# Two-layer hybrid backbone: the prologue of the first norm rewritten, with the first scale rows of the modulation computed on TensorE

## The reference, cut to what matters

```python
sc_lat = jax.nn.silu(c)
sc_ctx = jax.nn.silu(c_ctx)
for l in range(DEPTH):
    ml = adaln_chunks(sc_lat @ w_mod[l] + b_mod[l])      # 9 chunks of 1024
    mc = adaln_chunks(sc_ctx @ w_mod[l] + b_mod[l])
    xl = xl + 0.5 * ml[2] * swiglu(modulate(rms_norm(xl, norm_ffn1[l]), ml[0], ml[1]), ffn1_w13[l], ffn1_w2[l])
    xc = xc + 0.5 * mc[2] * swiglu(modulate(rms_norm(xc, norm_ffn1[l]), mc[0], mc[1]), ffn1_w13[l], ffn1_w2[l])
    ...
# modulate(h, shift, scale) = h * (1 + scale) + shift
```

## Time and profile before

| | us |
|---|---|
| median of three runs | 1928.98 |
| the profiled execution's own time | 1927.45 |
| its span in the profile | 1925.8 |
| PE busy with matmuls | 1762.3 (92%) |
| DVE busy | 1434.1 (74%) |
| ACT busy | 734.0 (38%) |

### The profile page before, as it was taken

How to read it: one execution, slowest core, us unless ns; L and a number is a source line. 1 busy time by engine, 2 the same in 40 slices (tenths; PEclk the granted TensorE clock), 3 DMA queues, 4 the chain that set the end, 5 groups by cost and what they waited for, 6 DMA issues and landing times.

```text
span 1925.8 us, 25366 instructions
## 1 busy us (share of the span) xinstructions
PE 1762.3 (92%) x9004; PEld 1444.1 (75%) x9004; DVE 1434.1 (74%) x2341; ACT 734.0 (38%) x1072; POOL 49.7 (3%) x97
## 2 busy tenths in 40 slices
PE   0699999998898898999999979999999799879999
PEld 0488888876676466788888858888887578569999
DVE  6888787887778666877777666878786778756766
ACT  3422222226646656222222262222223764654342
POOL 0000000000000000000000000000000000000000
PEclk9999999998999898999999989999999899889999
DMA  8544444422212013544444323444430321125453
GB/s 321 196 175 160 167 150 176 141 79 110 99 44 110 1 75 136 207 151 166 161 154 171 115 85 131 174 152 164 163 142 34 125 97 63 73 110 172 177 174 109
DMA packets 36859, 260.44 MB, mean 135 GB/s; under 512 B 4288, under 2 KB 5632, under 8 KB 6080
## 3 DMA queue, kind: packets, MB, share of 16 engines
q1 hardware_dynamic: 25920, 183.34, 26.4%
q0 software_dynamic: 10880, 76.32, 11.0%
HBM read 253.62 MB, written 5.24 MB: 134 GB/s over the span
## 4 chain that ended last, share of the span: by engine, by line
PE 79%; DVE 8%; ACT 8%; issue 2%; DMA 2%; POOL 0%; DVEq 0%; ACTq 0%; SPq 0%; POOLq 0%
PE ps L1304 24%; PE ps L1305 24%; PE ps L1306 24%; DVE mod_prod L856 3%; ACT n_t L543 2%; PE ps L1370 1%; ACT h_hi L546 1%; PE ps L1577 1%; DMA mod_raw<-mod_in 1%; DVE x_res L937 1%; ACT w_hi L501 1%; DVE w_lo L833 1%; PE ps L1542 1%; ACT w_hi L508 1%; DVE w_lo L838 1%
## 5 line engine op out<-in xcount | busy, mean ns | idle before, releaser
L1304 PE MATMUL ps<-h_hi,w_hi 128*128 128x512 f32 (+1 forms) x1872 | 691.8, 370 | 75.7 <-DVE h_lo L908 66.2
L1305 PE MATMUL ps<-h_lo,w_hi 128*128 128x512 f32 (+1 forms) x1872 | 686.0, 366 | 0.0
L1306 PE MATMUL ps<-h_hi,w_lo 128*128 128x512 f32 (+1 forms) x1872 | 685.3, 366 | 0.0
L1304 PEld LDWEIGHTS ps<-h_hi,w_hi 128*128 128x128 f32 x1872 | 357.6, 191 | 148.7 <-issue 71.9
L1306 PEld LDWEIGHTS ps<-h_hi,w_lo 128*128 128x128 f32 x1872 | 357.3, 191 | 58.4
L1305 PEld LDWEIGHTS ps<-h_lo,w_hi 128*128 128x128 f32 x1872 | 357.8, 191 | 56.4 <-issue 0.2
L937 DVE SCALAR_TENSOR_TENSOR x_res<-ps,abg,x_res 128x256 f32<-128x256 f32 x640 | 272.1, 478 | 155.7 <-PE ps L1306 154.9
L833 DVE TENSOR_TENSOR w_lo<-raw,w_hi 128x2048 fp32r<-128x2048 f32 x132 | 302.0, 2288 | 87.6 <-ACT w_hi L501 87.5
L501 ACT ACTIVATE w_hi<-raw 128x2048 fp32r<-128x2048 f32 x132 | 252.3, 1912 | 270.1 <-PE ps L1306 259.2
L856 DVE CUSTOM_DVE_ANT_0 mod_prod<-mod_raw,cb 128x1024 f32<-128x1024 f32 x288 | 338.7, 1220 | 15.3 <-DMA mod_raw<-mod_in 13.6
L1304 PE MATMUL ps<-a_hi,w_hi 128*128 128x512 f32 (+1 forms) x640 | 232.3, 363 | 2.2 <-DVE x_res L937 2.2
(11 more groups left out here) (189 smaller groups left out, 1322.3 us busy)
## 6 DMA issues: line engine op xcount, KB each, us to landing
raw<-ffn_in SPq DMA_DIRECT2D x132, 1024.0 KB, 4.8
mod_raw<-mod_in POOLq DMA_DIRECT2D x72, 1024.0 KB, 5.1
raw<-proj_in SPq DMA_DIRECT2D x20, 1024.0 KB, 4.9
raw<-out_w_in SPq DMA_DIRECT2D x8, 1024.0 KB, 6.5
x_spill<-x_res SPq DMA_DIRECT2D x2, 2048.0 KB, 7.2
x_res<-x_spill SPq DMA_DIRECT2D x2, 2048.0 KB, 8.1
cb<-c_in SPq DMA_DIRECT2D x2, 1024.0 KB, 4.7
x_res<-x_in SPq DMA_DIRECT2D x1, 2048.0 KB, 11.9
```

Of the source, the lines that this page charges most:

```text
L1304: pe.matmul(dst, w_hi[:, slot, wsl], hi, start=first, stop=False)
L1305: pe.matmul(dst, w_hi[:, slot, wsl], lo, start=False, stop=False)
L1306: return pe.matmul(dst, w_lo[:, slot, wsl], hi, start=False, stop=last)
```

## The change

Nothing is changed in the arithmetic of the loops. The prologue is rewritten:

- The eight scale tiles of the first norm are computed on TensorE: `scale_in` holds 8 tiles of 128 x 1024 (0.5 MB each), `scale_tile(j)` is 8 float32 matmuls with 128 x 128 weights and 2 moving columns (`cond`, Silu of 16 new columns of `cols`). They use two new half-size buffers and `sg`, `gu`.
- The eight shift tiles stay on DVE, as pieces 0 and 1 of the new `mod_in` (pieces are renumbered, there are two fewer). POOL queues: both halves of piece 0, scale tiles 0 to 3, both halves of piece 1 (each waits for half of piece 0's products), scale tiles 4 to 7. `MOD_PRE` is now pieces 2 and 3; piece 2 is computed at the end of the prologue and piece 3 in `ffn_phase(0)`. The loops have one piece for each turn as before.
- `cb` comes as one row (8 KB) and is broadcast by four float32 matmuls of 512 columns with a row of ones as weights; ACT applies Silu from PSUM.
- The sum of squares is accumulated by eight float32 matmuls with the mean matrix instead of seven DVE additions and one matmul.
- SP brings 260 columns of constants first, `x_res` in two halves, and no longer waits before the weight units. The other constants follow behind the units of FFN 0 (`const_rest`), the masks behind the write of `x_res` in the mixer; ACT rounds the masks in step `R.3` of layer 0.
- DVE takes shift, scale, root product and remainder two channel tiles at a time, with products of the later pieces between. PE takes slot 0 and slot 1 for a channel tile one behind the other (`first_pair`), scale tiles 4 to 7 between them; ACT's splits of the three slots lie inside the norm.

```diff
-            for q in range(*MOD_START):
-                load_piece(q)
+            load_half(0, 0)
+            load_half(0, 1)
+            for j in range(4):
+                load_scale(j)
+            load_half(1, 0)
+            load_half(1, 1)
+            for j in range(4, KT):
+                load_scale(j)
...
-            for slot in range(3):
-                split(slot, 0, 0)
             act.wait_ge(const_in_s, 16)
-            norm_rest(0, T)
+            norm_rest(0, T, {-1: lambda: split(0, 0, 0), 1: lambda: split(1, 0, 0), 5: lambda: split(2, 0, 0)})
...
-            dve.wait_ge(cb_ready, 2)
-            mod_pieces(0, 1)
-            for d in range(1, KT):
-                add_square(0, d, T)
-            mod_pieces(1, MOD_START[1] - 1)
-            split(0, 0, 0)
-            dve.wait_ge(cols_in_s, 16)
-            derive(0, "ab")
...
+            dve.wait_ge(cb_ready, 2)
+            products(0, 0, 0)
+            dve.wait_ge(cb_ready, 4)
+            products(0, 0, 1)
+            dve.wait_ge(cols_in_s, 16)
+            shift_half(0)
+            products(0, 1, 0)
+            products(0, 1, 1)
+            shift_half(1)
+            split(0, 0, 0)
+            scale_half(0)
+            scaled(0)
+            scaled(1)
+            dve.wait_ge(mod_put, 1)
+            products(1, 0, 0)
+            first_remainder(0)
+            first_remainder(1)
+            scale_half(1)
+            scaled(2)
+            scaled(3)
+            split(1, 0, 0)
+            first_remainder(2)
+            first_remainder(3)
+            products(1, 0, 1)
+            shift_half(2)
+            scale_half(2)
+            scaled(4)
+            scaled(5)
+            products(1, 1, 0)
+            first_remainder(4)
+            first_remainder(5)
+            products(1, 1, 1)
+            shift_half(3)
+            scale_half(3)
+            scaled(6)
+            scaled(7)
+            mod_tile(2, 0)
+            first_remainder(6)
+            first_remainder(7)
+            for j in range(1, 4):
+                mod_tile(2, j)
+            split(2, 0, 0)
...
+            def scale_tile(j):
+                pe.wait_ge(scale_in_s[j % 4], 16 * (j // 4) + 16)
...
+                for k in range(KT):
+                    last = pe.matmul(ps[:, 4 + j // 2, 2 * (j % 2):2 * (j % 2) + 2], w[:, P * k:P * k + P], cond[:, k, :], start=(k == 0), stop=(k == KT - 1))
+                last.then_inc(scale_mm, 1)
...
+            condition_rows()
+            first_mean()
+            for j in range(4):
+                scale_tile(j)
+            first_pair(0, 0)
+            first_pair(0, 1)
+            scale_tile(4)
+            scale_tile(5)
+            first_pair(1, 0)
+            first_pair(1, 1)
+            scale_tile(6)
+            scale_tile(7)
+            for k in range(2, KT):
+                for unit in range(2):
+                    first_pair(unit, k)
```

More of the change, by code:

```diff
@@ L127, in backbone @@
         lam = sb(ctx, "lam", [96])
+        cond = sb(ctx, "cond", [KT, 2])
         sel_r = sb(ctx, "sel_r", [8, P], F32R)
@@ L617, in mixer @@
                         decay_rows(layer, j)
+                        if layer == 0 and j == 3:
+                            act.wait_ge(masks_in_s, 16)
+                            act.activation(const_r[:, :], cexp[:, :, :].rearrange("p h t -> p (h t)")[:, 0:N_MASKS], ACT.Copy).then_inc(masks_done, 1)
                     elif kind == "si":
@@ new lines, in scaled, with first_remainder, products @@
+            def scaled(d):
+                dve.wait_ge(rstd_done, 2)
+                if d >= 2:
+                    dve.wait_ge(h_lo_s, d - 1)
+                tt(n_t[:, d % 2, :], x_res[:, d, :], n_rstd[:, :], ALU.mult).then_inc(t_done, 1)
+            def first_remainder(d):
+                dve.wait_ge(h_hi_s, d + 1)
+                tt(h_lo[:, d, :], n_t[:, d % 2, :], h_hi[:, d, :], ALU.subtract).then_inc(h_lo_s, 1)
+            def products(q, half, s):
+                if s == 0:
+                    dve.wait_ge(mod_in_s[half], 16 * q + 16)
+                for jj in range(2):
+                    done = 8 * q + 4 * half + 2 * s + jj
+                    if done >= 2:
+                        dve.wait_ge(mod_step, done - 1)
+                    j = 2 * half + jj
+                    dve.tensor_tensor_reduce(mod_prod[:, jj], mod_raw[:, half, jj], cb[:, s, :], 1.0, 0.0, ALU.mult,
+                                             ALU.add, mod_acc[:, s, j:j + 1]).then_inc(mod_step, 1)
+                if half == 1 and s == 1:
+                    dve.wait_ge(mod_step, 8 * q + 8)
+                    dve.tensor_copy(mod_t[:, :, 4 * q + KT:4 * q + KT + 4], mod_acc[:, :, :]).then_inc(mod_put, 1)
@@ L1615, in out_part, with condition_rows, first_mean, first_pair @@
                     x.then_inc(unit_done if m % 2 else o_mm, 1)
-            mean(0, T)
+            def condition_rows():
+                pe.wait_ge(one_s, 1)
+                pe.wait_ge(cb_in_s, 16)
+                for s in range(2):
+                    for part in range(2):
+                        pe.matmul(ps[:, 4 + 2 * s + part, :], n_rstd[0:1, 0:P], cb[0:1, s, 512 * part:512 * part + 512],
+                                  start=True, stop=True).then_inc(cond_rows, 1)
+            def first_mean():
+                pe.wait_ge(const_in_s, 16)
+                for d in range(KT):
+                    pe.wait_ge(sq_done, d + 1)
+                    pe.matmul(ps[:, 0, :], c_(K_MEAN, P), n_t[:, d % 2, :] if d else n_acc[:, :], start=(d == 0),
+                              stop=(d == KT - 1)).then_inc(mean_done if d == KT - 1 else acc_done, 1)
+            def scale_tile(j):
+                pe.wait_ge(scale_in_s[j % 4], 16 * (j // 4) + 16)
+                if j == 0:
+                    pe.wait_ge(cond_cols, 1)
+                    pe.wait_ge(cb_ready, 4)
+                w = scale_w[:, j % 4, :] if j % 4 < 2 else (sg, gu)[j % 2][:, :, :].rearrange("p s t -> p (s t)")
+                for k in range(KT):
+                    last = pe.matmul(ps[:, 4 + j // 2, 2 * (j % 2):2 * (j % 2) + 2], w[:, P * k:P * k + P], cond[:, k, :], start=(k == 0), stop=(k == KT - 1))
+                last.then_inc(scale_mm, 1)
+            def first_pair(unit, k):
+                if k == 0:
+                    split_ready(unit, 0)
+                pe.wait_ge(h_lo_s, k + 1)
+                for m in range(2):
+                    last = mm3(ps[:, 2 * unit + m, :], unit, slice(256 * k + P * m, 256 * k + P * m + P), hk(k, T), T, k == 0, k == KT - 1)
+                if k == KT - 1:
+                    last.then_inc(unit_done, 1)
+            condition_rows()
[13 more added lines that the diff above has]
+                    first_pair(unit, k)
             for layer in range(DEPTH):
```

108 lines of the change are left out of this document (74 added, 34 removed).

## The result

| | before | after |
|---|---|---|
| median of five runs, us | 1928.81 (1927.88 to 1929.27) | 1916.31 (1911.58 to 1921.08) |
| ratio, 95% interval | | 0.9937 [0.9919, 0.9955] |
| the same kernel a second time, us | | 1913.30 (1911.43 to 1921.42), 0.9918 [0.9905, 0.9932] |
| profiled execution, us | 1927.45 | 1920.51 |
| its span, us | 1925.8 | 1918.8 |

They scatter over 10 us; the five of before scatter over 1.4, and the 27 of before that were timed beside e5 over 4.4. The profiled execution is one of the slow ends of that scatter.

The account below looks back on a forecast made before the run. The prologue's DVE chain, which TensorE waits for, was taken as the bound; shortening it gives at most 26.7 us, TensorE's slow clock cuts this to 22, so 1928.98 - 22 = 1907 us, range 1900 to 1919.

Parts of the forecast that it names:

- rivals 1 and 3: 1: TensorE slow through the prologue, 1914 to 1920 us, chance 0.18; 3: transfers late, 1909 to 1915 us, chance 0.10.
- the likeliest case: Whole kernel: a gain of 22 us (18 to 25), giving 1907 us; chance 0.48.
- the point of comparison: Start of the fifth tile of `down`, 109.48 us before; what follows was taken as unchanged, so its lead is the gain.
- The rule from DVE's split of slot 0 to the fifth tile: End of prologue to fifth tile of `down`: 19.4 us, from 20.5 us before less 1.06 of waiting for TensorE.
- the rival without a stall on TensorE: Prologue: the DVE chain alone is last, a gain of 26.7 us, 1902 us; chance 0.16.
- The most it could give: DVE chain: from 29.5, 33.9 us without waiting, then 19.4, puts the fifth tile at 82.8, a gain of 26.7 us.
- 4.7 for TensorE: Prologue: TensorE's lateness in ending unit 0, between the 26.7 us of the DVE chain and the forecast gain of 22.
- the middle: TensorE in the prologue: 22 us, between a gain of 24.3 and one of 18 to 21 with early work mostly slow.
- The row that it leaned on: Prologue before: after 35 us of idleness, matmuls start 0.43 us apart from 65.39 to 71.50, a slow start costing 3.0 us.
- The other row: Mixer before: 16 small matmuls run at the fast pace, the large ones right behind them start 0.42 us apart.
- Rival 1: Prologue: TensorE stays slow, three `scale_half` steps wait 2 to 4 us each; gain 9 to 15, 1914 to 1920 us; chance 0.18.
- The wrong release: Prologue: the DMA of piece 1's first half was to release `products(1, 0, 0)` near 29.5 us, expected at 28 to 33.

Follow-up runs that it names:

- e5: The changed kernel with each scale tile one matmul instead of eight, leaving out seven eighths of the first scale's contraction: 1902.9 us, ratio 0.9863.
- e6: The kernel before with one idle DVE memset of 0.91 us ahead of its first norm products: 1929.28 us, ratio 1.0004.
- e7: The kernel before with two idle DVE memsets (1.76 and 0.91 us) ahead of its first norm products: 1931.7 us, ratio 1.0014.
- e2: The changed kernel with 64 moving columns instead of 2 in the scale tiles' matmuls, same result: 1912.66 us, ratio 0.9917.
- e8: The kernel before with only the masks' DMA and rounding moved into the mixer of layer 0: 1929.34 us, ratio 1.0001.
- e10: e9 with the first half of piece 1 queued behind two scale tiles instead of four and computed ahead of the split of slot 0: 1911.37 us, 0.9913.
- e9: e4 with the first half of x_res ahead of cols on SP, and the Silu of cond behind those of cb: 1908.48 us, 0.9901.
- e3: The changed kernel with the first half of piece 3 computed ahead of the first FFN phase's split of slot 0: 1912.62 us, ratio 0.9907.
- e12: The changed kernel with an idle DVE memset of 1.76 us ahead of derive(0, "g"): 1919.22 us, ratio 0.9955.
- e4: The changed kernel with the edits of both e2 and e3: 1908.68 us, ratio 0.9899; again 1909.68 us, 0.9898.

## Why the prediction was right, point by point

The prediction was 1907 us with 1900 to 1919; the two measurements, 1916.3 and 1913.3, lie within it, in the part that belonged to rivals 1 and 3. The sign and the mechanism held, the size of the likeliest case (a gain of 22) did not: 17.1 us at the point of comparison, 14.5 behind it, 12 to 16 at the end. Of the way from 22 to the end only the first step, to 17.1, is one that the forecast had weighed; that the losses behind it still left the time within the range is luck.

**What held.** The bound was read rightly: by e6 and e7 a delay in the prologue passes one for one to the end. For gains this held less well. By the ratio the changed kernel ends 2.3 us short of its lead at the first mixer load in one measurement and 2.3 beyond it in the other; the forms made from it that keep the full result end 3.5 to 6.4 short. The rule from DVE's split of slot 0 to the fifth tile, 19.4 us from the earlier trace rows, came out as 72.98 to 92.35, 19.37, and as 19.38 in e2. The first FFN matmul started at 35.19 (31 to 36 was given), the split of slot 0 for the norm at 27.40 with its end at 29.7 (26.5 to 30.5), the scale tiles at 1.9 to 3.55 (1.5 to 3.4). Masks and late constants cost nothing that can be seen: the lead at the first mixer load and at the write of `x_res` is the same 14.5 us, and e8 measures the masks alone. e5 is the rival without a stall on TensorE, 1902.9 us where 1902 was given. DVE's work was sized well: 33.9 us up to the end of the prologue, and in the changed kernel 36.8 from 31.21 to 68.03 with 2.9 of waiting in it. That the time agrees so closely is in part luck: e5's split of slot 0 comes at 65.7, not 63.4, its lead at the first mixer is 24.5 and not 26.7, and its layer 1 was one of the fast ones.

**The sum, term by term.** The most it could give was 26.7 us with DVE never waiting from 29.5 on. `products(1, 0, 0)` started at 31.21, 1.7 later. The three waits in `scale_half` took 2.9, and the wait for unit 0 took 4.95: 26.7 - 1.7 - 2.9 - 4.95 = 17.1, the measured lead. The forecast had put 4.7 for TensorE, where 7.8 were lost; of those e2 gives back 4.7.

**The mis-sized term: the slow level.** The forecast took "the middle" between a TensorE that recovers by itself in 15 matmuls and one that is slow to tile 4. The row that it leaned on, 6.1 us of slow matmuls behind 35 us of idleness, had only full matmuls behind it. The other row, small matmuls with slow full ones behind the earlier trace rows, was the nearer one: TensorE was at 0.50 in 30 to 40 and 45 to 50 us with no gap at all, and fell back to it in tiles 4 and 5. The Trainium skill (TensorE: Matmul & The Clock Gate, Part 1: The HAM clock gate) says that the throttled state is the default and activity releases it; the trace agrees in so far as with matmuls of 2 columns without a gap the clock fell to 0.50 and with those of 64 columns it stayed at 1.00 (25 to 30 us in e2). Rival 1 was thus the right mechanism at less than its price: it gave 9 to 15 us, since it counted 2 to 4 us for each of three waits that took 0.45, 1.14 and 1.28.

**A reading that does not stand.** The forecast took a granted clock of 1.00 beside full matmuls 0.43 us apart as a sign that the slow pace behind 35 us of idleness is not what the throttle takes. In the changed kernel full matmuls that start 0.43 apart stand beside 0.50 each time (35 to 40, 45 to 50 and 92.3 to 97.3 us). So the 1.00 of that one stretch of before is no proof of full pace; the distance between starts is the surer sign. The sum is not touched by it, since it took its prices from the starts.

**The wrong release.** The forecast let the DMA set the start of `products(1, 0, 0)`, near 29.5. The row at 31.21 has no wait: DVE came from the split of slot 0, which had waited 7.56 us for ACT behind the mean. By e10, the transfer of the half piece is there at 25.7 when it is favoured; in the changed kernel its own landing is hidden, so that it was at 31.2 or earlier is all that can be said. The mean's chain starts at 12.93, when the first half of x has landed; in the first 5 us the core moved 146 GB/s, in the kernel before 238. From then on TensorE sets the pace: ACT's fourth square waits 2.96 us for it, and each one after that 0.23 to 1.07. The first line is a window of the kernel before, the second ACT's row in the changed one:

```profile
0.00:5.00 5.00, 0.00 (x0) 1.00 0.67 238
```

```profile
17.55 0.63 ACT L557 ACTIVATE n_t<-x_res 128x512 f32<-128x512 f32 x1 [2.96 <-PE ps L1737]
```

e9, in which the order of the first transfers is another, has the same wait of 2.96 us and gains nothing.

**What was not foreseen.** First, filler work that hid a wait. Piece 4 before lay ahead of DVE's split of slot 0; the change renumbers the pieces and leaves that place empty, so the 4.95 us were idle and piece 3's products came later, whole, ahead of the update that TensorE waits for. e3 takes that back (6.9 us at the first mixer load). Second, behind the wait of 4.46 us before the fifth tile TensorE was at its slow level: it ran at full pace until 87.50, and the twelve matmuls behind the wait run at the slow pace, 0.43 us from start to start. This is the timeline of the changed kernel:

```profile
87.50 0.39 PE L1414 MATMUL ps<-a_hi,w_lo 128*128 128x512 f32 x1
...
97.21 0.63 PE L1414 MATMUL ps<-a_hi,w_lo 128*128 128x512 f32 x1
97.64 0.53 PE L1412 MATMUL ps<-a_hi,w_hi 128*128 128x512 f32 x1
```

At 0.43 instead of 0.227 that is 2.5 us, which is the fall of the lead from 17.1 to 14.5. The point of comparison was taken one wait too early. In e2, with a wait of 4.44 us, two matmuls are fast, the next eight slow, and the lead falls by 1.6; in e12, with a wait of 6.42, eight are slow and it falls by 1.6; in e4, whose wait is 2.62 us, and in e3, which has no wait, it doesn't fall. The Trainium skill (TensorE: Matmul & The Clock Gate, Part 1: The HAM clock gate) adds that the count of slow matmuls differs between runs of one kernel and that the penalty is under 1% of a typical span. The first is not seen here: both traces of the changed kernel have twelve, and the counts of 12 and 8 are of different forms. The second agrees, 2.5 us of 1919, but that is a sixth of this change's gain.

**What stays open.** The loss in layer 1, 7 us in the profiled execution. That the time is lost where the granted clock is lower, in unaltered code and without idle time, is shown (the windows above, and e12), and among timed executions of the changed kernel the slowest have the lowest mean clock; seven of ten lose less than the profiled ones (1911 to 1916 us against 1920.5 and 1921.4). Why kernels with the same instructions in layer 1 come to the second mixer with another level is not settled. The forecast took it for granted that a microsecond gained stays gained; by the ratios that holds within about 6 us here.

## What to carry to other kernels

A matrix-vector product moved to TensorE is nearly all weight load. Here 64 moving columns in place of 2 cost nothing in the tile itself (1.95 us, against 1.93 at full pace and 3.55 at the slow one) and kept the clock up for the tiles and for the full matmuls behind them. When a change takes work out of a queue, look at what that work was hiding: a wait behind it comes into view, and the next piece should be split across the hole. Where a kernel's time scatters by 10 us, judge by landmarks in the traces and by several executions, not by one span.

## What the runs showed of the hardware

- TensorE with no gap between instructions sat at its lower level: 0.50 over 30 to 40 and 45 to 50 us with matmuls of 2 and 512 columns mixed; 1.00 in 25 to 30 and 45 to 50 us with 64 in place of 2 (e2). In tiles 4 and 5 it fell from full to slow pace without idle time.
- The weight loads of such tiles followed the level: 16 records took 3.55 us at 0.50; at full pace they took 1.93 us with 2 columns and 1.95 with 64.
- A wait of 4.46 us behind full matmuls at 1.00 was followed by twelve slow matmuls, one of 6.42 us (e12) and one of 4.44 us (e2) by eight, one of 2.62 us (e4) by none.
- A granted clock of 1.00 stood beside full matmuls 0.43 us apart at 65 to 70 us of the kernel before.
- The same code of the second mixer ran with a granted clock between 0.67 and 0.93 over 20 us, and from the second write to the output the forms differed by 7 us.
- The core moved 146 GB/s in the first 5 us, with small rows and one megabyte of x in the queues, and 419 to 430 from 5 to 35 us.
